# First unit of a differential attention begun before the last tile of the projection in front of it

## The chip, the cores and the metric

One Trainium2 chip, one of its cores. The whole computation is one program; the metric is its time on the device in microseconds, the median of several executions. A change of less than 0.2% (3.9 us here) cannot be told from none with these runs.

## The reference, cut to what matters

Two transformer blocks in fp32 over a sequence of 512 tokens and a width of 1024. The first block (an mLSTM layer and a sparse-attention layer) is not touched. The second block projects the normed input once and feeds two branches from it, an RWKV7 scan and a differential attention:

```python
u = h @ w_in[i]
u_rwkv = u[..., :RWKV_COLS]                       # 1920 columns
u_da = u[..., RWKV_COLS:RWKV_COLS + DA_COLS]      # 1536 columns
...
u = u + mu_prev * (up[:, :-2] - u) + mu_next * (up[:, 2:] - u)      # centred_shift, RWKV columns only
a = sigmoid(a0 + ad @ a2); decay = exp(-exp(-softplus(-(w0 + tanh(wd) @ w2)) - 0.5))
...
lam = exp(sum(lq1 * lk1)) - exp(sum(lq2 * lk2)) + lambda_init
s = einsum('bhcqd,bhckd->bhcqk', q_blk, kt)       # 4 heads, c = 2 score maps, blocks of 128 queries
pr = softmax(s, axis=-1)
pd = pr[:, :, 0] - lam * pr[:, :, 1]
o = einsum('bhqk,bhkv->bhqv', pd, vt)
```

Then come the RWKV scan, both output projections, a feed-forward layer and a gated per-layer embedding.

## The kernel before, in words

Each engine has its own list of instructions, written out in order in Python, and engines meet only at semaphores. `stage_in_2` (the third in-projection) and `stage_da_attention` lie in the same block, so that no barrier stands between them.

**The projection.** The weights stream in as blocks of 256 output columns (the last has 128). ScalarE makes the high part of a block (`split_hi`, L248), VectorE the low part (`split_lo`, L257), and TensorE multiplies 128 columns at a time, a tile, as three products with 24 matmuls (`multiply_tile`). There are 43 tiles, t = 0 to 42; tile number modulo 4 gives the PSUM bank. Tiles t = 28 to 42 are the 15 RWKV tiles, v = 0 to 14. VectorE takes each of these out of its bank with the root of the norm (L2158), releases the bank (L2160), and computes the centred shift in three instructions (L2162, L2163, L2165). The last two tiles are t = 41 (v = 13, bank 2) and t = 42 (v = 14, bank 3), so banks 0 and 1 are free by then.

**What is put between the tiles.** After t = 40 and t = 41 TensorE makes the first head pair's decay and rate products (`first_pass_lora`, L2048), two matmuls each. ScalarE takes their sigmoids (`rw_sigmoids`, L2444), with VectorE's two cumulative scans (`rw_scans`, L2479) in front of the last tile's eviction. GpSimd then multiplies keys by the rate (L2289), and after the wait for `lam` makes sums and differences of the scans (L2294, L2298, L2303) and the key scales (L2308, L2314).

**The attention.** A unit n is a head and a block of 128 queries, 16 in all. TensorE makes both score maps in banks 2 (n mod 2) and the next (`scores`, L2236); VectorE takes both maxima in one reduction (L2382); ScalarE makes both exponentials with their sums (L2351); VectorE inverts the sums (L2394), makes the scalar with lambda (L2395) and the difference of the maps (L2397), which releases TensorE's transposes (L2257), ScalarE's copy (L2358) and the products with V (L2269). VectorE's order is maximum n, then the difference of unit n - 1. TensorE's scores n wait for the exponentials of unit n - 2. Between the units n = 3 to 7 ScalarE makes ten exponentials of the RWKV branch, two at a time, and GpSimd multiplies with them; `beside(m)` lets GpSimd go on only after m differences.

Before the change VectorE's list at the seam reads: eviction 13, shift 13, scans, eviction 14, shift 14, two tiny instructions for `neg_lam` (L2189, L2190), maximum 0, maximum 1, difference 0, maximum 2, difference 1. TensorE's: tile 41, lora 1, tile 42, scores 0, scores 1, scores 2 and so on. ScalarE's: sigmoids 0, sigmoids 1, exponentials 0.

Of the kernel before, what the change touches and what calls it, by code (L numbers as in the profile page):

```python
# [31 lines left out]
DA_HEADS = 4  # L32
# [5 lines left out]
LAMBDA_INIT = 0.8 - 0.6  # L38
# [37 lines left out]
BLOCK_AT, TILE_AT = [], []  # L76
# [1841 lines left out]
RW_ALL = 15  # L1918


def stage_in_2(k, norm):
    nc = k.nc
    b0 = first_block("in_2")
# [22 lines left out]
          "lam_mm", "exp", "copied", "squares", "sums", "floor", "half", "rinv", "wide", "turned", "kkn", "lam", "tanh")}  # L1946
    k.dap, k.rw_done = s, rw_done
    rw_tensors(k)
    first_lora = k.const("cos", S).rearrange("p (m c) -> p m c", m=4)
    k.scan_landed, lora_landed = k.sem("rw_scan_landed"), k.sem("rw_first_lora_landed")  # L1950
    swapped, cleared = [k.sem(f"dap_swapped{i}") for i in range(2)], k.sem("dap_turned_cleared")
# [5 lines left out]
    with k.joined() as block:  # L1957
# [30 lines left out]
        @block.scalar  # L1988
        def _(act):
            split_hi(k, act, b0 + 1)  # L1990
            norm.take_root(act)
            for t, (b, j) in enumerate(tiles):
                if t and j == 0 and b + 1 < b1:
                    split_hi(k, act, b + 1)
                c = t - K0 - 1
                if 0 <= c < RW_T:
                    act.wait_ge(rw_done, made[4 + c])
                    if c >= 2:
                        act.wait_ge(s["sums"], c - 1)
# [80 lines left out]
        def _(dve):  # L2080
# [49 lines left out]
            for t, (b, j) in enumerate(tiles):  # L2130
# [25 lines left out]
                else:  # L2156
                    m = place[v]
                    dve.tensor_tensor(u[:, v % 2, 1:1 + S], bank, norm.root[:], ALU.mult).then_inc(u_ready, 1)  # L2158
                    dve.wait_ge(u_ready, v + 1)
                    dve.sem_inc(k.evac_done, 1)  # L2160
                    x = u[:, v % 2]
                    steps.then_wait(dve, dve.tensor_scalar(t1[:, 0], x[:, 1:1 + S], k.keep[:, m:m + 1], None, ALU.mult))  # L2162
                    steps.then_wait(dve, dve.scalar_tensor_tensor(out=t1[:, 1], in0=x[:, 0:S], scalar=k.col("mu_prev", m),  # L2163
# [21 lines left out]
                    rope(n)  # L2185
                if 8 <= n < 12:
                    value(n - 8)
            dve.wait_ge(s["exp"], 1)
            steps.then_wait(dve, dve.tensor_tensor(prod[:, 4:5], prod[:, 3:4], prod[:, 2:3], ALU.subtract))  # L2189
            dve.tensor_scalar(k.neg_lam, prod[:, 4:5], -LAMBDA_INIT, None, ALU.add).then_inc(s["lam"], 1)  # L2190

def stage_da_attention(k):
    nc = k.nc
    k.da_o = k.region("da_o", [P, TT, S], F32, 74)
    p = k.at("da_p", [P, 3, 2, S], F32, 60)
    pt = k.at("da_pt", [P, 2, S], F32, 72)
    junk = k.region("da_junk", [P, 2, P], F32, 71.25)
    s = {n: k.sem(f"daa_{n}") for n in (  # L2200
          "sc_mm", "nm_done", "exp_done", "pd_done", "tr_mm", "pt", "pv_mm",
          "o_done", "sq_done", "step", "rw_landed", "root", "y_tr", "y_hi", "gate",
          "y_lo", "normed", "omk", "bh")}
    units = [(h, i) for h in range(DA_HEADS) for i in range(TT)]
    U = len(units)
    sumsq = k.small[:, 64:64 + U]
    k.daa, k.da_sumsq = s, sumsq
# [9 lines left out]
    def sm(base, n):  # L2217
        return k.small[:, base + 2 * (n % 4):base + 2 * (n % 4) + 2]

    with k.joined() as block:  # L2220
        @block.sync
# [5 lines left out]

        @block.tensor
        def _(pe):
            def scores(n):  # L2230
                h, i = units[n]
                if n >= 2:
                    pe.wait_ge(s["exp_done"], 2 * (n - 1))
                for c in range(2):
                    rows = rows_half(c)
                    last = pe.matmul(k.ps[:, 2 * (n % 2) + c, :], k.da[rows, h, i * P:(i + 1) * P],  # L2236
                                     k.da[rows, DA_HEADS + h, :], start=True, stop=True)
                last.then_inc(s["sc_mm"], 1)

            pe.wait_ge(k.dap["done"], 8)  # L2240
            pe.wait_ge(k.dap["tr_read"], 4)
            pe.wait_ge(k.evac_done, TILE_AT[b1] - 2)
            scores(0)
            for n in range(U + 3):
                if n == 0:
                    pe.wait_ge(k.evac_done, TILE_AT[b1])
                if n + 1 < U:
                    scores(n + 1)
# [25 lines left out]
        def _(pool):  # L2274
# [66 lines left out]
        def _(act):  # L2341
            exponentials = [x for d in range(2) for x in rw_exponentials(k, act, 0, d)]
            for n in range(U + 4):
                if n < U:
                    act.wait_ge(s["nm_done"], n + 1)
                    if n >= 3:
                        act.wait_ge(s["tr_mm"], n - 2)
                    if n >= 4:
                        act.wait_ge(s["pd_done"], n - 3)
                    for c in range(2):  # L2350
                        act.activation(p[:, n % 3, c, :], k.ps[:, 2 * (n % 2) + c, :], ACT.Exp, bias=sm(0, n)[:, c:c + 1],  # L2351
                                       accum_out=sm(8, n)[:, c:c + 1]).then_inc(s["exp_done"], 1)
                if 2 <= n < U + 2:
                    m = n - 2
                    act.wait_ge(s["tr_mm"], m + 1)
# [15 lines left out]

        @block.vector
        def _(dve):
            steps = Steps(s["step"])
            dve.wait_ge(k.dap["lam"], 1)
            for n in range(U + 4):
                if n < U:
                    bank = 2 * (n % 2)
                    dve.wait_ge(s["sc_mm"], n + 1)
                    if n >= 4:  # L2380
                        dve.wait_ge(s["exp_done"], 2 * (n - 3))
                    dve.tensor_reduce(sm(0, n), k.ps[:, bank:bank + 2, :], AX, ALU.max, negate=True) \  # L2382
                        .then_inc(s["nm_done"], 1)
                if n >= 4:
                    m = n - 4
                    h, i = units[m]
                    dve.wait_ge(s["pv_mm"], m + 1)
                    dve.tensor_scalar(k.da_o[:, i, h * P:(h + 1) * P], k.ps[:, 6 + m % 2, 0:P], sm(24, m)[:, 0:1], None,
                                      ALU.mult).then_inc(s["o_done"], 1)
                if 1 <= n <= U:  # L2390
                    m = n - 1
                    dve.wait_ge(s["exp_done"], 2 * m + 2)
                    x, w = p[:, m % 3], sm(24, m)
                    steps.then_wait(dve, dve.reciprocal(w, sm(8, m)))  # L2394
                    steps.then_wait(dve, dve.scalar_tensor_tensor(out=sm(32, m)[:, 0:1], in0=w[:, 1:2], scalar=k.neg_lam,  # L2395
                                                                  in1=sm(8, m)[:, 0:1], op0=ALU.mult, op1=ALU.mult))
                    dve.scalar_tensor_tensor(out=x[:, 0, :], in0=x[:, 1, :], scalar=sm(32, m)[:, 0:1], in1=x[:, 0, :],  # L2397
                                             op0=ALU.mult, op1=ALU.add).then_inc(s["pd_done"], 1)


def halves():
# [4 lines left out]
def rows_half(x):  # L2406
    return slice(64 * x, 64 * x + 64)
# [1250 lines left out]
```

## Time and profile before

| | |
|---|---|
| median of three runs | 1936.8 us (1934.7 to 1937.28) |
| profiled execution, its own time | 1933.06 us |
| its span, first to last instruction | 1931.1 us |
| mean granted TensorE clock | 0.989 of full speed |
| TensorE matmuls busy | 1851.7 us, 96% of the span |
| VectorE, ScalarE, GpSimd busy | 57%, 36%, 11% |
| the seam of the two stages, last eviction to first transposes | 1088.27 to 1097.68 us |
| the attention's maxima | 1091.6 to 1131.0 us |

The table says how full the engines are over the whole program. The busy shares are means over stages whose limits differ, so that the seam has to be read by itself, engine by engine, in order of time.

### The profile page before, as it was taken

The numbers are of one execution on the slowest core, as the hardware profiler recorded it, in microseconds if no ns is written. First come the engines' busy times: TensorE is split into PE (matmuls) and PEld (weight loads), VectorE is DVE, ScalarE is ACT, GpSimd is POOL, SyncE is SP. The second block draws the span as 40 slices with busy tenths as digits, with TensorE's granted clock in tenths as the row PEclk, the third lists the DMA queues.
The fourth block names the chain that finished last, engine by engine and source line by source line (L and its number), as shares of the span: only waits on it lengthen the run. The fifth ranks groups of instructions, "written<-read, shape, count | busy, mean of one in ns | idle before, by whom it ended". The sixth has DMA issues, their size and how long they took to land. (4 is left out here: it accounts for less than half of the span.)

```text
span 1931.1 us, 35675 instructions
## 1 busy us (share of the span) xinstructions
PE 1851.7 (96%) x15284; PEld 1484.9 (77%) x15284; DVE 1097.6 (57%) x1648; ACT 693.0 (36%) x1154; POOL 221.5 (11%) x221
## 2 busy tenths in 40 slices
PE   8999999999999899999999899999899999999996
PEld 7887757688887666778888568878878888888875
DVE  4664354563256777444366887777465635354534
ACT  4325332341223787442212473423233322122342
POOL 4210011140002000210021340000001000000011
PEclk9999999999999999999999999999999999999998
DMA  5334323152224010124321100002042322322121
GB/s 187 115 109 142 130 77 116 44 209 99 69 69 141 3 45 2 67 92 141 125 100 55 47 2 4 4 3 69 4 175 90 107 98 90 106 92 105 55 98 44
DMA packets 42379, 160.73 MB, mean 83 GB/s; under 512 B 4976, under 2 KB 14192, under 8 KB 27632
## 3 DMA queue, kind: packets, MB, share of 16 engines
q1 hardware_dynamic: 28016, 143.78, 21.7%
q10 hardware_dynamic: 14208, 14.68, 2.1%
q8 instruction: 122, 2.00, 0.4%
q14 instruction: 33, 0.27, 0.0%
HBM read 140.36 MB, written 16.78 MB: 81 GB/s over the span
## 5 line engine op out<-in xcount | busy, mean ns | idle before, releaser
L257 DVE TENSOR_TENSOR wlo<-raw,whi 128x2048 fp32r<-128x2048 f32 (+2 forms) x113 | 251.4, 2225 | 183.9 <-ACT whi L248 183.6
L248 ACT ACTIVATE whi<-raw 128x2048 fp32r<-128x2048 f32 (+2 forms) x113 | 209.0, 1850 | 317.9 <-PE ps L283 161.4
L281 PE MATMUL ps<-act_hi,whi 128*128 128x512 f32 x616 | 243.6, 395 | 0.0
L301 PE MATMUL ps<-act_lo,whi 128*128 128x512 f32 x632 | 242.0, 392 | 0.0
L283 PE MATMUL ps<-act_hi,wlo 128*128 128x512 f32 x616 | 240.8, 391 | 0.0
L282 PE MATMUL ps<-act_lo,whi 128*128 128x512 f32 x616 | 240.7, 391 | 0.0
L300 PE MATMUL ps<-act_hi,whi 128*128 128x512 f32 x592 | 235.5, 398 | 0.0
L305 PE MATMUL ps<-act_hi,wlo 128*128 128x512 f32 x632 | 156.5, 389 | 0.0
L301 PEld LDWEIGHTS ps<-act_lo,whi 128*128 128x128 f32 x632 | 119.7, 189 | 25.6 <-issue 1.2
L305 PEld LDWEIGHTS ps<-act_hi,wlo 128*128 128x128 f32 x632 | 118.6, 188 | 24.6
L300 PEld LDWEIGHTS ps<-act_hi,whi 128*128 128x128 f32 x592 | 111.1, 188 | 32.2 <-issue 8.1
L283 PEld LDWEIGHTS ps<-act_hi,wlo 128*128 128x128 f32 x616 | 116.3, 189 | 24.6
L281 PEld LDWEIGHTS ps<-act_hi,whi 128*128 128x128 f32 x616 | 116.4, 189 | 24.3 <-issue 0.5
L282 PEld LDWEIGHTS ps<-act_lo,whi 128*128 128x128 f32 x616 | 116.2, 189 | 24.1 <-issue 0.5
L3329 PE MATMUL ps<-f_hi,wlo 128*128 128x512 f32 x256 | 99.6, 389 | 0.0
L3328 PE MATMUL ps<-f_lo,whi 128*128 128x512 f32 x256 | 99.6, 389 | 0.0
L3327 PE MATMUL ps<-f_hi,whi 128*128 128x512 f32 x256 | 99.6, 389 | 0.0
L1830 ACT ACTIVATE att_p<-ps,small 128x512 f32<-128x512 f32 (+3 forms) x128 | 66.3, 524 | 28.0 <-DVE small L1871 27.6
L3361 DVE TENSOR_TENSOR xT<-xT,ps 128x512 f32<-128x512 f32 x32 | 21.9, 686 | 82.6 <-PE ps L3329 82.6
L3297 ACT ACTIVATE f_hi<-ff_sq 128x512 fp32r<-128x512 f32 x32 | 20.2, 633 | 123.1 <-DVE ff_sq L3352 123.1
L1871 DVE TENSOR_REDUCE small<-ps 128x2 f32<-128x1024 f32 (+3 forms) x64 | 52.5, 820 | 19.4 <-PE ps L1769 19.2
L1783 PE MATMUL ps<-consts,att_p 128*128 128x128 f32 x320 | 50.7, 285 | 12.0 <-ACT att_p L1837 8.3
(520 smaller groups left out, 3362.0 us busy)
## 6 DMA issues: line engine op xcount, KB each, us to landing
raw<-stream_in SPq DMA_DIRECT2D x107, 1024.0 KB, 4.9
v_scratch<-v_out ACTq DMA_DIRECT2D x16, 256.0 KB, 3.3
z_scratch<-zt ACTq DMA_DIRECT2D x16, 256.0 KB, 2.9
mlh_v<-v_scratch SPq DMA_DIRECT2D x4, 1024.0 KB, 4.8
mlh_z<-z_scratch SPq DMA_DIRECT2D x16, 256.0 KB, 2.6
cmp_w<-cmp_w_in SPq DMA_DIRECT2D x2, 2048.0 KB, 11.3
z_scratch<-in_zt ACTq DMA_DIRECT2D x16, 256.0 KB, 2.2
mix_g<-z_scratch SPq DMA_DIRECT2D x16, 256.0 KB, 6.9
```

Source lines behind the costliest of these rows:

```text
L248: act.activation(k.whi[b % 2][:, 0:n], k.raw[b % RAW_SLOTS][:, 0:n], ACT.Copy).then_inc(k.hi_done, 1)
L257: dve.tensor_tensor(k.wlo[b % 2][:, 0:n], k.raw[b % RAW_SLOTS][:, 0:n], k.whi[b % 2][:, 0:n].bitcast(F32), ALU.subtract).then_inc(k.lo_don ...
L281: pe.matmul(bank, hi, x_hi, start=(x == 0), stop=False)
L282: pe.matmul(bank, hi, x_lo, start=False, stop=False)
L283: last = pe.matmul(bank, lo, x_hi, start=False, stop=(x == end))
L300: pe.matmul(bank, hi, x_hi, start=(x == 0), stop=False)
L301: pe.matmul(bank, hi, x_lo, start=False, stop=False)
L305: last = pe.matmul(bank, lo, x_hi, start=False, stop=(x == end))
L1830: act.activation(p[:, n % 3, e, 0:L], k.ps[:, 2 * (n % 2) + e, 0:L], ACT.Exp, bias=sm(0, n)[:, e:e + 1], accum_out=sm(8, n)[:, e:e + 1]).t ...
L3327: pe.matmul(k.ps[:, t % 4, :], whi, f_hi[:, kt, :], start=(kt == 0), stop=False)
L3328: pe.matmul(k.ps[:, t % 4, :], whi, f_lo[:, kt, :], start=False, stop=False)
L3329: last = pe.matmul(k.ps[:, t % 4, :], wlo, f_hi[:, kt, :], start=False, stop=(kt == KD - 1))
```

## The change

Unit 0 of the attention is begun in the projection. TensorE makes scores 0 after tile 41 and before lora 1, behind waits for the rotated queries and keys, the turned values and the eviction of tile 40. VectorE takes maximum 0 after eviction 13 and before shift 13; `neg_lam` is made after eviction 12; difference 0 and maximum 1 stand between eviction 14 and shift 14. ScalarE makes exponentials 0 between the two pairs of sigmoids, behind a wait for all weight splits, because the tile `da_p` lies over the weight buffers. GpSimd waits for the last tile's matmuls instead of for `lam`. The helper functions are the old bodies of the attention's loops, moved to the top level.

```diff
+def da_weights(k, act, n):
+    act.wait_ge(k.daa["nm_done"], n + 1)
...
+    for c in range(2):
+        act.activation(k.da_p[:, n % 3, c, :], k.ps[:, 2 * (n % 2) + c, :], ACT.Exp, bias=da_small(k, 0, n)[:, c:c + 1],
+                       accum_out=da_small(k, 8, n)[:, c:c + 1]).then_inc(k.daa["exp_done"], 1)
...
@@ stage_in_2, scalar
                     act.wait_ge(k.lo_done, b1 - 2)
+                    if m:
+                        act.wait_ge(k.lo_done, b1)
+                        da_weights(k, act, 0)
                     rw_sigmoids(k, act, 0, m, (4 + 2 * m, 5 + 2 * m))
@@ stage_in_2, tensor
                 multiply_tile(k, pe, b, j, norm if t == 0 else None)
+                if t == K0 + RW_ALL - 2:
+                    pe.wait_ge(s["done"], 8)
+                    pe.wait_ge(s["tr_read"], 4)
+                    pe.wait_ge(k.evac_done, TILE_AT[b1] - 2)
+                    da_scores(k, pe, 0)
@@ stage_in_2, vector
                     dve.sem_inc(k.evac_done, 1)
+                    if v == RW_ALL - 3:
+                        dve.wait_ge(s["exp"], 1)
+                        steps.then_wait(dve, dve.tensor_tensor(prod[:, 4:5], prod[:, 3:4], prod[:, 2:3], ALU.subtract))
+                        dve.tensor_scalar(k.neg_lam, prod[:, 4:5], -LAMBDA_INIT, None, ALU.add).then_inc(s["lam"], 1)
+                    if v == RW_ALL - 2:
+                        da_maximum(k, dve, 0)
+                    if v == RW_ALL - 1:
+                        dve.wait_ge(s["lam"], 1)
+                        da_difference(k, dve, 0)
+                        da_maximum(k, dve, 1)
@@ stage_da_attention, tensor
-            scores(0)
             for n in range(U + 3):
@@ stage_da_attention, gpsimd
-            pool.wait_ge(k.dap["lam"], 1)
+            pool.wait_ge(k.tile_done, TILE_AT[b1])
             past(pool, "scan", 2)
@@ stage_da_attention, scalar
-                if n < U:
+                if 0 < n < U:
@@ stage_da_attention, vector
-                if n < U:
+                if 2 <= n < U:
...
-                if 1 <= n <= U:
+                if 2 <= n <= U:
```

## Rows read from the trace of the kernel before

**Rows 1.** The page, busy time of an engine, share, instructions.

```profile
PE 1851.7 (96%) x15284; PEld 1484.9 (77%) x15284; DVE 1097.6 (57%) x1648; ACT 693.0 (36%) x1154; POOL 221.5 (11%) x221
```

**Rows 2.** By stretch: busy PE, PEld, DVE, ACT, POOL; granted clock, DMA share, GB/s.

```profile
1096.00:1100.00 4.00, 3.29 (x12) 1.17 (x10) 3.93 (x6) 1.93 (x5) 3.77 (x5) 0.72 0.00 2
...
1108.00:1116.00 8.00, 7.34 (x47) 4.68 (x46) 7.79 (x17) 8.00 (x26) 4.11 (x4) 1.00 0.00 0
```

**Rows 3.** Timeline of TensorE over the seam.

```profile
1080.90 1.88 PE L2048 MATMUL ps<-rw,consts 128*128 128x512 f32 x4
...
1088.16 2.04 PE L2236 MATMUL ps<-da 64*128 64x512 f32 x8
1094.34 3.41 PE L2236 MATMUL ps<-da 64*128 64x512 f32 x8 [4.14 <-ACT da_p L2351]
```

**Rows 4.** Timeline of VectorE over the seam.

```profile
1081.10 0.69 DVE L2158 TENSOR_TENSOR in_u<-ps,norm_mix_root 128x512 f32<-128x512 f32 x1 [2.83 <-PE ps L283]
...
1084.94 3.31 DVE L2479 TENSOR_TENSOR_SCAN rw_first_X<-consts,rw_first_sig 128x512 f32<-128x512 f32 x2
1088.27 0.69 DVE L2158 TENSOR_TENSOR in_u<-ps,norm_mix_root 128x512 f32<-128x512 f32 x1
1089.11 0.49 DVE L2162 TENSOR_SCALAR in_t<-in_u,mu_keep 128x512 f32<-128x512 f32 x1
...
1091.20 0.16 DVE L2189 TENSOR_TENSOR da_prod<-da_prod 128x1 f32<-128x1 f32 x1
...
1091.58 2.36 DVE L2382 TENSOR_REDUCE small<-ps 128x2 f32<-128x1024 f32 x2
1094.32 0.17 DVE L2394 RECIPROCAL small<-small 128x2 f32<-128x2 f32 x1 [0.38 <-ACT da_p L2351]
...
1096.58 1.21 DVE L2382 TENSOR_REDUCE small<-ps 128x2 f32<-128x1024 f32 x1
...
1099.24 1.22 DVE L2382 TENSOR_REDUCE small<-ps 128x2 f32<-128x1024 f32 x1
```

**Rows 5.** Timeline of ScalarE over the seam.

```profile
1074.83 1.28 ACT L2444 ACT_TABLE_LOAD   x1 [6.15 <-PE ps L2048]
1076.13 1.26 ACT L2444 ACTIVATE rw_first_sig<-ps,cols 128x512 f32<-128x512 f32 x2
1082.02 1.49 ACT L2444 ACTIVATE rw_rate<-ps,cols 128x512 f32<-128x512 f32 x2 [4.63 <-PE ps L2048]
1083.52 1.28 ACT L2351 ACT_TABLE_LOAD   x1
...
1100.49 0.69 ACT L2351 ACTIVATE da_p<-ps,small 128x512 f32<-128x512 f32 x1 [0.74 <-DVE small L2382]
```

**Rows 6.** By line, duration in ns min/median/max.

```profile
L2165 DVE SCALAR_TENSOR_TENSOR rw<-in_u,cols,in_t x15: 751/752/1661, 1003.5 to 1090.4; 128x512 f32<-128x512 f32 x15
...
L2395 DVE SCALAR_TENSOR_TENSOR small<-small x16: 219/219/1260, 1094.5 to 1134.0; 128x1 f32<-128x1 f32 x16
...
L2397 DVE SCALAR_TENSOR_TENSOR da_p<-da_p,small x16: 750/752/1493, 1095.2 to 1134.2; 128x512 f32<-128x512 f32 x16
```

**Rows 7.** Timeline of VectorE and GpSimd in the projection, of GpSimd over the seam.

```profile
975.78 2.29 DVE L257 TENSOR_TENSOR wlo<-raw,whi 128x2048 fp32r<-128x2048 f32 x1
...
976.01 3.21 POOL L1981 TENSOR_TENSOR da_straight<-da,consts 128x512 f32<-128x512 f32 x1 [4.15 <-DVE da L2100]
...
1082.88 3.18 POOL L2289 TENSOR_TENSOR rw_b<-rw_kkn,rw_rate 128x512 f32<-128x512 f32 x2 [32.51 <-ACT rw_rate L2444]
1091.63 2.48 POOL L2294 TENSOR_TENSOR rw_first_E<-rw_first_X,rw_first_sig 128x512 f32<-128x512 f32 x2 [5.57 <-DVE small L2190]
1094.07 2.04 POOL L2298 TENSOR_TENSOR rw_first_E<-rw_first_X 128x512 f32<-128x512 f32 x2
1096.25 1.52 POOL L2303 TENSOR_TENSOR rw_first_X<-rw_first_E,rw_first_sig 128x512 f32<-128x512 f32 x1
1097.77 2.03 POOL L2308 TENSOR_SCALAR rw_rate<-rw_rate,cols,small 128x512 f32<-128x512 f32 x2
```

More of the change, by code:

```diff
@@ L1918, with da_tensors, da_small, da_scores @@
 RW_ALL = 15
+def da_tensors(k):
+    k.daa = {n: k.sem(f"daa_{n}") for n in (
+          "sc_mm", "nm_done", "exp_done", "pd_done", "tr_mm", "pt", "pv_mm",
+          "o_done", "sq_done", "step", "rw_landed", "root", "y_tr", "y_hi", "gate",
+          "y_lo", "normed", "omk", "bh")}
+    k.da_p = k.at("da_p", [P, 3, 2, S], F32, 60)
+    k.da_steps = Steps(k.daa["step"])
+def da_small(k, base, n):
+    return k.small[:, base + 2 * (n % 4):base + 2 * (n % 4) + 2]
+def da_scores(k, pe, n):
+    h, i = n // TT, n % TT
+    if n >= 2:
+        pe.wait_ge(k.daa["exp_done"], 2 * (n - 1))
+    for c in range(2):
+        rows = rows_half(c)
+        last = pe.matmul(k.ps[:, 2 * (n % 2) + c, :], k.da[rows, h, i * P:(i + 1) * P],
+                         k.da[rows, DA_HEADS + h, :], start=True, stop=True)
+    last.then_inc(k.daa["sc_mm"], 1)
+def da_maximum(k, dve, n):
+    bank = 2 * (n % 2)
+    dve.wait_ge(k.daa["sc_mm"], n + 1)
+    if n >= 4:
+        dve.wait_ge(k.daa["exp_done"], 2 * (n - 3))
+    dve.tensor_reduce(da_small(k, 0, n), k.ps[:, bank:bank + 2, :], AX, ALU.max, negate=True) \
+        .then_inc(k.daa["nm_done"], 1)
+def da_weights(k, act, n):
+    act.wait_ge(k.daa["nm_done"], n + 1)
+    if n >= 3:
+        act.wait_ge(k.daa["tr_mm"], n - 2)
+    if n >= 4:
+        act.wait_ge(k.daa["pd_done"], n - 3)
+    for c in range(2):
+        act.activation(k.da_p[:, n % 3, c, :], k.ps[:, 2 * (n % 2) + c, :], ACT.Exp, bias=da_small(k, 0, n)[:, c:c + 1],
+                       accum_out=da_small(k, 8, n)[:, c:c + 1]).then_inc(k.daa["exp_done"], 1)
+def da_difference(k, dve, m):
+    dve.wait_ge(k.daa["exp_done"], 2 * m + 2)
+    x, w = k.da_p[:, m % 3], da_small(k, 24, m)
+    k.da_steps.then_wait(dve, dve.reciprocal(w, da_small(k, 8, m)))
+    k.da_steps.then_wait(dve, dve.scalar_tensor_tensor(out=da_small(k, 32, m)[:, 0:1], in0=w[:, 1:2], scalar=k.neg_lam,
+                                                       in1=da_small(k, 8, m)[:, 0:1], op0=ALU.mult, op1=ALU.mult))
+    dve.scalar_tensor_tensor(out=x[:, 0, :], in0=x[:, 1, :], scalar=da_small(k, 32, m)[:, 0:1], in1=x[:, 0, :],
+                             op0=ALU.mult, op1=ALU.add).then_inc(k.daa["pd_done"], 1)
 def stage_in_2(k, norm):
@@ L1948, in stage_in_2 @@
     rw_tensors(k)
+    da_tensors(k)
     first_lora = k.const("cos", S).rearrange("p (m c) -> p m c", m=4)
@@ L2187, in _ @@
                     value(n - 8)
-            dve.wait_ge(s["exp"], 1)
-            steps.then_wait(dve, dve.tensor_tensor(prod[:, 4:5], prod[:, 3:4], prod[:, 2:3], ALU.subtract))
-            dve.tensor_scalar(k.neg_lam, prod[:, 4:5], -LAMBDA_INIT, None, ALU.add).then_inc(s["lam"], 1)
 def stage_da_attention(k):
@@ L2196, in stage_da_attention @@
     k.da_o = k.region("da_o", [P, TT, S], F32, 74)
-    p = k.at("da_p", [P, 3, 2, S], F32, 60)
+    p = k.da_p
     pt = k.at("da_pt", [P, 2, S], F32, 72)
     junk = k.region("da_junk", [P, 2, P], F32, 71.25)
[L2200 to L2203, printed above, removed]
+    s = k.daa
     units = [(h, i) for h in range(DA_HEADS) for i in range(TT)]
@@ L2206, in stage_da_attention @@
     sumsq = k.small[:, 64:64 + U]
-    k.daa, k.da_sumsq = s, sumsq
+    k.da_sumsq = sumsq
     b1 = first_block("mix_o")
@@ L2215, in stage_da_attention @@
     k.da_scale = k.small[:, 97:98]
-    def sm(base, n):
-        return k.small[:, base + 2 * (n % 4):base + 2 * (n % 4) + 2]
     with k.joined() as block:
@@ L2229, in _ @@
         def _(pe):
[L2230 to L2242, printed above, removed]
-            scores(0)
             for n in range(U + 3):
@@ L2247, in _ @@
                 if n + 1 < U:
-                    scores(n + 1)
+                    da_scores(k, pe, n + 1)
                 if 2 <= n < U + 2:
@@ L2343, in _ @@
             for n in range(U + 4):
-                if n < U:
[L2345 to L2352, printed above, removed]
+                if 0 < n < U:
+                    da_weights(k, act, n)
                 if 2 <= n < U + 2:
@@ L2373, in _ @@
         def _(dve):
-            steps = Steps(s["step"])
-            dve.wait_ge(k.dap["lam"], 1)
             for n in range(U + 4):
-                if n < U:
[L2378 to L2383, printed above, removed]
+                if 2 <= n < U:
+                    da_maximum(k, dve, n)
                 if n >= 4:
@@ L2387, in _ @@
                     dve.wait_ge(s["pv_mm"], m + 1)
-                    dve.tensor_scalar(k.da_o[:, i, h * P:(h + 1) * P], k.ps[:, 6 + m % 2, 0:P], sm(24, m)[:, 0:1], None,
+                    dve.tensor_scalar(k.da_o[:, i, h * P:(h + 1) * P], k.ps[:, 6 + m % 2, 0:P], da_small(k, 24, m)[:, 0:1], None,
                                       ALU.mult).then_inc(s["o_done"], 1)
-                if 1 <= n <= U:
[L2391 to L2398, printed above, removed]
+                if 2 <= n <= U:
+                    da_difference(k, dve, n - 1)
 def halves():
```

## The prediction

> **What bounds the kernel now.** I read the page first, for the shares: TensorE's matmuls are busy 96% of the span, VectorE 57% and ScalarE 36% [rows 1]. By the page alone, work on VectorE or ScalarE looks free. But the chain of waits that the page follows back covers only the program's last quarter and does not reach the seam, so it says nothing on this change. The timelines of the engines over the seam, one by one, do.
>
> TensorE's timeline shows a hole: it makes scores 0 and 1 from 1088.16, and scores 2 come only after 4.14 us in which it waited for the first exponentials [rows 3]. What is late is seen on VectorE: from 1088.27 it is never idle but for 0.38 us until it reaches maximum 2 at 1096.58. It evicts the last tile, shifts it, makes lambda, and only at 1091.58 starts the first maximum [rows 4]. So VectorE sets the start of the attention. In front of eviction 13 it was idle 2.83 us [rows 4], which is cover. The table by stretch shows who takes over: from 1108 to 1116 ScalarE is busy 8.00 of 8 us, VectorE 7.79 [rows 2]. ScalarE starts exponentials 3 at 1100.49, after a wait of 0.74 for maximum 3 [rows 5], and is nearly full from there. So **the time of maximum 3 (1099.24) is the one to follow**: what it moves, the whole attention moves, and the RWKV stage behind it, which begins with the attention's last products.
>
> **The change, part by part.**
>
> *TensorE.* Two scores cost 2.04, so scores 0 cost 1.02 [rows 3]. They leave the attention and lie in front of lora 1 and the last tile. None of their waits holds: VectorE, idle before eviction 13, had finished all that they ask for. The last tile ends 1.02 later, and with it eviction 14: 1088.27 becomes 1089.29. This price is certain, since TensorE is full up to there. The three table loads by DMA that start at the last tile's end start 1.0 later too; they are wanted only after the last maximum, over 30 us on, so nothing.
>
> *VectorE in front of eviction 14.* Maximum 0 (2.36 / 2 = 1.18 [rows 4]) starts when scores 0 end, about 1082.1, a wait of some 0.2 behind eviction 13, and ends at 1083.3. Queued behind it is shift 13 (2.1 us, as 1089.11 to 1091.20 [rows 4]), to 1085.4, then the scans. Even at the 3.31 that they took here they end at 1088.7, under the last tile's matmuls. So maximum 0 costs nothing where it is put; if that cover failed by more than 0.6 us it would show. Lambda's 0.38 (1091.20 to 1091.58) goes into the idle 2.83: nothing.
>
> *VectorE behind it.* Before, from eviction 14 to maximum 2: 0.84 eviction, 2.09 shift, 0.38 lambda, 2.74 for two maxima and the wait, 2.26 difference 0 (1094.32 to 1096.58), 8.31 in all [rows 4]. After: 0.84 eviction, difference 0 at 2.26, maximum 1 at 1.18, shift 2.09, together 6.37. With the 1.02 later start, maximum 2 is at 1088.27 + 1.02 + 6.37 = 1095.66, **0.92 us earlier**, as long as GpSimd disturbs no more than before.
>
> *ScalarE.* The exponentials need another table than the sigmoids. Before: one load for the sigmoids, one for the exponentials [rows 5]. After: sigmoids 0, load, exponentials 0, load, sigmoids 1, load: two loads more at 1.28 each. The sigmoid load stood idle until lora's product, thus behind a wait of its activation, where the later one ran ahead of its wait [rows 5]; with two waits in front of exponentials 0 as of the sigmoids I let the load follow maximum 0, at 1083.3. Then exponentials 0 run from 1084.6 to 1086.0, a load to 1087.3, the first sigmoid of the rate to 1088.0. Before, GpSimd's first product began at 1082.88 [rows 7]; now at 1088.1. Should the load run ahead, all this is 1.3 us earlier. The third load (1088.8 to 1090.1) lies under the eviction.
> The Trainium skill (ScalarE: Activation LUTs, What ACT_TABLE_LOAD costs) counts 1.28 us and a drain of 1.38 for each switch. The trace does not show the drain: 1074.83 + 1.28 = 1076.11 and the activation starts at 1076.13 [rows 5]. By the page GpSimd would start 2.8 later, with the same clashes one turn on; the sum below would be an estimated +0.5 in place of +1.1.
>
> *GpSimd, and the lock.* This is what eats the gain. GpSimd and VectorE exclude each other: a GpSimd product that started at 976.01, inside the low split of 975.78 to 978.07, took 3.21, against 1.24 for one of two at 1091.63 [rows 7]. The other way, VectorE's operations with two inputs in SBUF waited: L2165 takes 0.75 but 1.66 beside L2289, L2395 0.22 but 1.26, L2397 0.75 but 1.49 [rows 6]. The maxima, which read PSUM, were not stretched (2.36 for two beside L2294 [rows 4, 7]). Before, L2294 waited 5.57 for lambda [rows 7], which stands behind shift 14, so that this shift had VectorE's ports for itself. After, it waits for the last tile only and comes right behind L2289, from about 1090.7. Its run of L2294, L2298, L2303 and L2308 (2.5, 2.0, 1.2, 1.5 undisturbed) now lies on difference 0, shift 14 and difference 1. Turn about: difference 0 ends at 1092.5, as slow as before. Maximum 1 to 1093.7, under L2294's second. Shift 14's first instruction ends at 1094.1; L2298 runs to 1095.1; the second ends at 1095.65; L2298's second runs to 1096.7; the third ends at 1097.25. Shift 14 takes 3.55 in place of 2.09: **+1.46**. Maximum 2 from 1097.3; difference 1 meets both L2308, 2.07 in place of 1.53 (1099.24 - 1096.58 - 1.13): **+0.54**. Maximum 3 at 1100.4.
> The Trainium skill (SBUF — State Buffer, on the shared port pair) has the loser block for the whole instruction. If each of the shift's three operations lost to a fresh 1.26 us one, that would be 3.8 in place of 1.46, and the sum an estimated +3.4.
>
> *Sum at maximum 3:* -0.92 + 1.46 + 0.54 = **+1.1 us**. The profiled execution took 1933.06 around a span of 1931.1, so it would be 1934.2; the median of the runs stands 3.7 above that execution, 1936.8 + 1.1 = **1937.9**.
>
> *Bounds.* Below: no clash on shift 14, and differences 0 and 1 at their free 1.14 (0.17 + 0.22 + 0.75): -0.92 - 1.12 - 0.4 = -2.4. Above: each of the shift's three loses 0.91 (the most of L2165) and difference 1 loses 1.04 + 0.74 in place of 0.4: -0.92 + 2.73 + 1.38 = +3.2.
>
> **The rivals.**
>
> *It gains a little* (0.31). GpSimd's run slips past shift 14, because VectorE holds the ports turn after turn or because L2289 lies elsewhere. For it: in the first kernel most of the 16 differences are at their minimum [rows 6]. Against it: GpSimd was busy without a pause from 1091.63 to 1099.8 [rows 7] and has the same to do. -0.9 to -2.4, 1935.2.
>
> *No change at all* (0.08). ScalarE's full stretch [rows 2] has its own start in its own queue, and a shift of maximum 3 by a microsecond is swallowed there. Against it: it still waited 0.74 for maximum 3 [rows 5]. 1936.8. That scores 0 have to wait after all, so that the change does nothing, is in here too.
>
> *It is slower by more than can be overlooked* (0.06). The clash doesn't end at difference 1: difference 2 loses 1.04 + 0.74 too, against the 0.4 it lost, so +3.2 + 1.4 = +4.6, 1941.4. It decides when VectorE's losses between eviction 14 and maximum 4 are over 5 us more than before. Against it: L2314 waits for differences and so can't start inside one.
>
> *It is faster by more than that* (0.05). TensorE's clock: the granted clock was 0.72 from 1096 to 1100 [rows 2], a mix of 2.4 and 1.2 GHz, after the 4.14 of idleness, and the scores of two units took 3.41 in place of 2.04 [rows 3]. With a shorter hole it could stay at 2.4 GHz: 1.4 more on top of the -2.4, 1933.0. Against it: the wait of TensorE on VectorE hides this today, so those 1.4 are hardly on the path.
>
> **How the numbers follow.** Forecast 0.50: 1937.9, by itself 1936.6 to 1939. The range for 8 in 10 takes in both bounds of the costs, 1934.4 and 1940.0, and some 0.4 for the median of a few runs: 1934.0 to 1940.4. Less than 0.2% of 1936.8 is 3.9 us, about what these runs can tell from no change. Forecast, small gain and no change are all inside: 0.89. Faster 0.05, slower 0.06.
>
> **What would show it.** Eviction 14 at 1.0 later than now, with idleness before it; maximum 0 between eviction 13 and shift 13; three table loads between the first sigmoids and exponentials 1; L2289 begun past 1087; L2294's on shift 14, whose three instructions are stretched to some 3.5 together; maximum 3 about 1 us later. A shift 14 of 2.1 shows me wrong towards the gain. A maximum 0 that pushes the scans past the last tile's end, or a hole in ScalarE behind exponentials 3, would show a step that I left out.

## The result, and the profile after

The change makes the kernel slower: median 1941.06 us over 18 runs against 1936.9 us over 18 runs of the kernel before on the same chip, ratio 1.0023, 95% interval 1.0016 to 1.0030. That is 4.2 us between the medians and 4.4 by the ratio (3.1 to 5.8), about the 3.9 that count as a difference, where 1937.9 (1934.0 to 1940.4) was forecast. The profiled execution took 1941.5 us, span 1939.6, clock 0.986. In the table below, one of e3's eleven executions, at 3102.6 us, is not in its ratio.

All figures below are microseconds counted from the start of eviction 13, the last of VectorE ahead of the change but for the two tiny ones for lambda, which now lie in the idleness in front of it (2.57 for 2.83), so that what lies ahead of it (1080.4 to 1084.5 us, from profile to profile) drops out. "The seam" ends with the attention's last eviction into `da_o`, at 56.62 before and at 60.75 after: **+4.13**, about what the medians differ by. The two profiles differ by another 4.9 behind the seam (793.4 and 798.3), but that part varies from 793.2 to 800.1 over the profiles of all kernels here, without an order that this change would explain.

VectorE's timeline after, from eviction 13 to maximum 5 (after the time: duration, line, operation, output<-inputs, shapes, and in brackets idleness and who ended it). It answers to [rows 4].

```profile
1080.59 0.69 DVE L2222 TENSOR_TENSOR in_u<-ps,norm_mix_root 128x512 f32<-128x512 f32 x1 [2.57 <-PE ps L283]
1081.66 1.22 DVE L1951 TENSOR_REDUCE small<-ps 128x2 f32<-128x1024 f32 x1 [0.38 <-PE ps L1941]
...
1089.04 0.69 DVE L2222 TENSOR_TENSOR in_u<-ps,norm_mix_root 128x512 f32<-128x512 f32 x1 [1.81 <-PE ps L305]
1090.30 0.17 DVE L1969 RECIPROCAL small<-small 128x2 f32<-128x2 f32 x1 [0.56 <-DVE in_u L2222]
1090.50 1.16 DVE L1970 SCALAR_TENSOR_TENSOR small<-small 128x1 f32<-128x1 f32 x1
1091.69 1.72 DVE L1972 SCALAR_TENSOR_TENSOR da_p<-da_p,small 128x512 f32<-128x512 f32 x1
1093.33 1.21 DVE L1951 TENSOR_REDUCE small<-ps 128x2 f32<-128x1024 f32 x1
1094.46 1.12 DVE L2236 TENSOR_SCALAR in_t<-in_u,mu_keep 128x512 f32<-128x512 f32 x1
1095.62 1.63 DVE L2237 SCALAR_TENSOR_TENSOR in_t<-in_u,cols,in_t 128x512 f32<-128x512 f32 x1
1097.29 1.14 DVE L2239 SCALAR_TENSOR_TENSOR rw<-in_u,cols,in_t 128x512 f32<-128x512 f32 x1
1098.67 1.23 DVE L1951 TENSOR_REDUCE small<-ps 128x2 f32<-128x1024 f32 x1 [0.23 <-DVE rw L2239]
...
1100.92 1.22 DVE L1951 TENSOR_REDUCE small<-ps 128x2 f32<-128x1024 f32 x1
...
1103.55 1.22 DVE L1951 TENSOR_REDUCE small<-ps 128x2 f32<-128x1024 f32 x1 [0.29 <-PE ps L1941]
1106.29 0.35 DVE L2425 TENSOR_SCALAR da_o<-ps,small 128x128 f32<-128x128 f32 x1 [1.52 <-PE ps L2320]
```

Between eviction 14 and maximum 3 (20.33 after eviction 13; 18.14 before) no idleness of VectorE names another engine: its own operations are long. L1970 takes 1.16 where it needs 0.22, L1972 1.72 for 0.75, and the shift's three 1.12, 1.63, 1.14 for 0.48, 0.75, 0.75. Behind maximum 3 it is the other way: its operations are short again and it waits 0.29 and 1.52 for TensorE. The two parts need two causes. GpSimd's timeline has the first; it answers to [rows 7]:

```profile
1087.90 2.51 POOL L2340 TENSOR_TENSOR rw_b<-rw_kkn,rw_rate 128x512 f32<-128x512 f32 x2 [38.03 <-ACT rw_rate L2474]
1090.37 2.48 POOL L2345 TENSOR_TENSOR rw_first_E<-rw_first_X,rw_first_sig 128x512 f32<-128x512 f32 x2
1092.81 2.49 POOL L2349 TENSOR_TENSOR rw_first_E<-rw_first_X 128x512 f32<-128x512 f32 x2
1095.44 1.26 POOL L2354 TENSOR_TENSOR rw_first_X<-rw_first_E,rw_first_sig 128x512 f32<-128x512 f32 x1
1096.70 2.38 POOL L2359 TENSOR_SCALAR rw_rate<-rw_rate,cols,small 128x512 f32<-128x512 f32 x2
```

It runs from 1087.90 to 1099.1 almost without a pause, over all five of the stretched operations, and ends before difference 1 (1099.81). The second cause is in the table by stretch, which answers to [rows 2] (busy PE, PEld, DVE, ACT, POOL; then the granted clock), and in TensorE's timeline, which answers to [rows 3]:

```profile
1092.00:1096.00 4.00, 0.00 (x0) 0.00 (x0) 3.96 (x4) 1.43 (x4) 3.86 (x4) 1.00 0.99 409
1096.00:1100.00 4.00, 2.52 (x8) 1.01 (x8) 3.69 (x4) 0.09 (x2) 3.07 (x3) 0.59 0.04 17
1100.00:1104.00 4.00, 2.58 (x7) 1.07 (x8) 3.60 (x7) 3.31 (x9) 1.93 (x2) 0.50 0.00 0
1104.00:1108.00 4.00, 4.00 (x19) 2.85 (x18) 2.41 (x6) 2.97 (x7) 0.60 (x1) 0.63 0.00 0
```

```profile
1096.07 1.48 PE L1941 MATMUL ps<-da 64*128 64x512 f32 x4 [4.24 <-ACT da_p L1962]
1097.48 1.11 PE L2308 MATMUL ps<-consts,da_p 128*128 128x128 f32 x4
1101.42 2.08 PE L1941 MATMUL ps<-da 64*128 64x512 f32 x4 [2.83 <-ACT da_p L1962]
1103.43 1.11 PE L2308 MATMUL ps<-consts,da_p 128*128 128x128 f32 x4
1104.34 1.91 PE L2320 MATMUL ps<-da_v,da_pt 128*128 128x128 f32 x8
1106.18 1.50 PE L1941 MATMUL ps<-da 64*128 64x512 f32 x4
...
1109.09 1.13 PE L1941 MATMUL ps<-da 64*128 64x512 f32 x4
...
1111.63 0.70 PE L1941 MATMUL ps<-da 64*128 64x512 f32 x2
```

TensorE stands idle 4.24, works 2.5, stands idle 2.83. From about 1096.7 to 1107.0, 10.2 us, it is at 1.2 GHz (0.50). There one unit takes it 4.76 from scores to scores (1101.42 to 1106.18), against 2.54 at 2.4 GHz (1109.09 to 1111.63). VectorE's own pace is 2.51 a unit (maximum 4 at 20.77 to maximum 5 at 23.28, before). At 2.4 GHz the two are level; at 1.2 GHz TensorE sets the pace.

The second hole ends with the exponentials of unit 2, which had waited for maximum 2 (1098.67).

ScalarE went as the prediction laid it out:

```profile
1082.98 1.28 ACT L1962 ACT_TABLE_LOAD   x1 [6.09 <-DVE small L1951]
...
1085.74 1.28 ACT L2474 ACT_TABLE_LOAD   x1
1087.04 1.27 ACT L2474 ACTIVATE rw_rate<-ps,cols 128x512 f32<-128x512 f32 x2
1088.32 1.28 ACT L1962 ACT_TABLE_LOAD   x1
```

### The profile page after: what moved, and what is told of

Read it like the earlier page. It is cut to its first block and busy times, and to the rows that moved or that the text cites. A ratio compares the mean times of both kernels' runs of the same rounds, so it can differ in the third digit from the quotient of the medians.

```text
span 1939.6 us, 35677 instructions
## 1 busy us (share of the span) xinstructions
PE 1855.8 (96%) x15284; PEld 1487.6 (77%) x15284; DVE 1098.1 (57%) x1648; ACT 695.5 (36%) x1156; POOL 221.4 (11%) x221
```

## The experiments

The table has what each run showed. The first three columns are of one profile each: maximum 3, the rest of the seam behind it, and the end. The last is the ratio to the kernel before, with its 95% interval; 0.001 is 1.9 us.

| kernel | to max 3 | from there | end | ratio |
|---|---|---|---|---|
| before | 18.14 | 38.48 | 56.62 | |
| before, again | 18.14 | 38.49 | 56.63 | 1.0001 [0.9992, 1.0011] |
| after | 20.33 | 40.42 | 60.75 | 1.0023 [1.0016, 1.0030] |
| after, again | 20.33 | 40.79 | 61.12 | one run, 1942.9 |
| e1 GpSimd behind shift 14 | 18.05 | 40.16 | 58.21 | 1.0007 [0.9998, 1.0016] |
| e2 sigmoids first | 20.13 | 39.56 | 59.69 | 1.0018 [1.0009, 1.0026] |
| e3 after, filler | 20.34 | 38.92 | 59.26 | 1.0021 [1.0012, 1.0029] |
| e4 before, GpSimd early | 20.25 | 38.48 | 58.73 | 1.0008 [0.9998, 1.0018] |
| e5 after, no reads | 16.51 | 38.48 | 54.99 | 0.9995 [0.9985, 1.0004] |
| e6 before, no reads | 17.35 | 38.48 | 55.83 | 1.0002 [0.9991, 1.0013] |
| e7 before, filler | 18.16 | 38.50 | 56.66 | 1.0012 [1.0003, 1.0022] |
| e9 one beside each | 16.50 | 40.36 | 56.86 | 1.0003 [0.9992, 1.0013] |
| e10 e1 and filler | 18.05 | 41.20 | 59.25 | one run, 1934.9 |
| e11 e9 and filler | 16.50 | 39.16 | 55.66 | 1.0005 [0.9994, 1.0016] |

**e1. When GpSimd starts.**

```diff
-            pool.wait_ge(k.tile_done, TILE_AT[b1])
+            pool.wait_ge(k.rw_done, RW_ALL)
```

> The changed kernel, with GpSimd's sums and differences of the scans held back until shift 14 is done (they waited for the last tile's matmuls). Theory 'lock': VectorE's maximum 2 is late because shift 14 takes turns with GpSimd at the shared ports; then shift 14 falls from 3.97 to about 2.1 us, maximum 2 comes some 2 us earlier, and of the 4.2 us of loss at least 2 go. Theory 'clock' adds that TensorE's waits become shorter, so that the stretch at 1.2 GHz gets shorter and 3 to 4 us go. Theory 'bare cost' (scores in front of the last tile, 1.0 us, and two more table loads, 2.6 us): nothing changes, 4 us stay.

With GpSimd's run begun only behind shift 14, difference 0 and the shift take their free times and maximum 2 is at 14.25 (15.48 before, 18.08 after). Then the rest of the run lies on differences 1 to 3; of difference 1:

```profile
1097.44 1.02 DVE L1970 SCALAR_TENSOR_TENSOR small<-small 128x1 f32<-128x1 f32 x1
1098.49 1.49 DVE L1972 SCALAR_TENSOR_TENSOR da_p<-da_p,small 128x512 f32<-128x512 f32 x1
```

The seam is 2.54 shorter than after's but still 1.59 longer than before's: the clash has moved, not gone. Its part behind maximum 3 (40.16) holds the losses of differences 2 and 3, and 1.2 GHz lasts 3.4 us, all of it ahead of maximum 3.

**e2. The table loads.** Both pairs of sigmoids in front of exponentials 0, so that ScalarE loads two tables in place of four.

```diff
+                    rw_sigmoids(k, act, 0, m, (4 + 2 * m, 5 + 2 * m))
                     if m:
                         act.wait_ge(k.lo_done, b1)
                         da_weights(k, act, 0)
-                    rw_sigmoids(k, act, 0, m, (4 + 2 * m, 5 + 2 * m))
```

> The changed kernel, with both pairs of sigmoids in front of exponentials 0, so that ScalarE loads two tables in place of four. Theory 'bare cost' (the table loads): 2.6 us of the 4.2 us come back. Theory 'lock': GpSimd's first product moves from 1087.9 to about 1084, so that difference 0 no longer meets it, but the sums and differences start at the last tile's end, 1089, and meet difference 0 and the first half of shift 14 in its place; VectorE loses nearly as much, 0 to 1.5 us come back. Theory 'clock': the waits of TensorE stay over 4 us, so the slow stretch stays; no more than 1.5 us back.

GpSimd's first product is early again (1084.86), as before the change, but its next ones come behind the scans and the last tile (1090.49) and lie on the same five operations. Maximum 3 gains 0.20, the end 1.06. So the loads are not what makes maximum 3 late. The other 0.86 lies behind it, where TensorE was at 1.2 GHz for 10.2 us, as in after; 0.37 of such a difference can be chance (e8 below), and the rest is not explained.

**e3 and e7. TensorE's clock.** Matmuls of constants, which nothing reads, in the holes: ten after (six in front of scores 3, four in front of scores 4), six before (in front of scores 2).

```diff
+            def filler(count):
+                pe.wait_ge(k.rw_ss["sigs"], 4)
+                for _ in range(count):
+                    pe.matmul(k.ps[:, 7, :], k.const("ident"), k.const("sin", S), start=True, stop=True)
...
+                if n in (2, 3):
+                    filler((0, 0, 6, 4)[n])
```

> The changed kernel with ten more matmuls of constants into an idle bank, six in front of scores 3 and four in front of scores 4, where TensorE waits for ScalarE; nothing reads them. Theory 'clock': the granted clock doesn't fall to 1.2 GHz between 1097 and 1106, the scores, transposes and products with V of the first units take 1.1, 0.7 and 1.1 us again, and about 1.9 us of the 4.2 come back; maximum 3 is where it was. Theory 'lock' alone: VectorE sets the pace and nothing comes back. 'Bare cost': nothing comes back. If the ten matmuls are longer than the waits that they fill, it is slower by the excess, at most 2 us.

> The kernel before with six matmuls of constants into an idle bank in front of scores 2, in TensorE's hole of 4.1 us; nothing reads them. Theory 'clock': the stretch at 1.2 GHz from 1095 to 1098.5 goes, and the attention gets at most 0.5 us shorter, because in this kernel VectorE, not TensorE, sets the pace through that stretch. If it gets 1.5 us or more shorter, the clock cost the kernel before as much as the changed one, and the clock explains none of the difference. Theory 'lock' alone: no change beyond 0.3 us.

The clock stays at 2.4 GHz in both. In e3:

```profile
1096.00:1100.00 4.00, 4.00 (x10) 1.71 (x9) 3.96 (x4) 1.45 (x4) 3.86 (x4) 1.00 0.99 398
1100.00:1104.00 4.00, 4.00 (x15) 1.72 (x14) 3.69 (x5) 0.17 (x1) 2.98 (x3) 1.00 0.02 9
1104.00:1108.00 4.00, 4.00 (x18) 1.77 (x17) 3.79 (x7) 3.37 (x10) 2.04 (x2) 1.00 0.00 0
```

After, maximum 3 doesn't move (20.34), and the part behind it falls from 40.42 to 38.92: 1.50 of the 1.94 come back. The fillers themselves are too long, 5.42 in the hole of 4.24 and 3.60 in that of 2.83, which may hold the rest. Before, the same cure gives nothing (56.66 for 56.62), as the prediction said of the kernel before. Its fillers too are longer than the hole (5.42 for 4.14), which could have eaten a small gain; but in before's own trace VectorE shows no wait for TensorE between eviction 14 and maximum 5, so that its time at 1.2 GHz is under VectorE's work. So the clock costs nothing before and some 1.5 after. The medians do not confirm a gain for either (below).

**e4. The new line of GpSimd alone**, in the kernel before.

```diff
-            pool.wait_ge(k.dap["lam"], 1)
+            pool.wait_ge(k.tile_done, TILE_AT[b1])
```

> The kernel before, with only the one line for GpSimd changed: its sums and differences wait for the last tile's matmuls and not for lambda. Theory 'lock': shift 14 goes from 2.1 to 3.5 to 4 us, the first maximum is that much later, and the kernel is 1.5 to 2 us slower; with 'clock' it may be 3. Against it, GpSimd is done sooner, so that difference 0 and difference 1 lose less than now, which gives back up to 1 us. 'Bare cost': no change, because neither the tile nor the table loads move.

+2.11 at maximum 3 and at the end. Shift 14's instructions show it:

```profile
1090.10 0.85 DVE L2162 TENSOR_SCALAR in_t<-in_u,mu_keep 128x512 f32<-128x512 f32 x1
1090.98 1.63 DVE L2163 SCALAR_TENSOR_TENSOR in_t<-in_u,cols,in_t 128x512 f32<-128x512 f32 x1
1092.65 1.41 DVE L2165 SCALAR_TENSOR_TENSOR rw<-in_u,cols,in_t 128x512 f32<-128x512 f32 x1
```

This one line, with the old order of everything else, costs about as much as the whole change does up to maximum 3 (+2.19). But not all of it is the clash. Differences 0 and 1 are free here, and VectorE then waits for scores 2, which TensorE makes at 1.2 GHz:

```profile
1097.95 3.79 PE L2236 MATMUL ps<-da 64*128 64x512 f32 x8 [6.76 <-ACT da_p L2351]
1100.08 1.22 DVE L2382 TENSOR_REDUCE small<-ps 128x2 f32<-128x1024 f32 x1 [0.94 <-PE ps L2236]
```

TensorE is at 1.2 GHz for 6.8 us, twice as long as before, and yet the part behind maximum 3 is 38.48 as before: how long the slow stretch lasts does not set the cost, but what it lies on.

**e5 and e6. The seam without the clash.** In both kernels eleven operations of GpSimd's (the products, sums and key scales up to `rw_kd`) are replaced by a memset of the same tile, which reads nothing and takes 0.5 in place of 1.2; the RWKV branch's first head pair thus gets constants. For one of them:

```diff
-                last = pool.tensor_tensor(E1[:, d, :], X[:, d, :], sig[:, d, :], ALU.subtract)
+                last = pool.memset(E1[:, d, :], 0.5)
```

> The changed kernel, with GpSimd's nine instructions between the sigmoids and the features (the products with the rate, sums and differences of the scans, key scales, scaled keys) replaced by fills of the same tiles with a constant, so that the RWKV branch is left out of the result; the fills read nothing and are short. It says what the change is worth where the ports are free. Counted from eviction 13 to the last eviction of the attention, which was 56.6 us before and 60.8 after. Theory 'lock': differences 0 to 3 and shift 14 at their free durations; maximum 2 at about 13.7 us behind eviction 13 (15.5 before), the last eviction at 53 to 55, and less than in the next kernel by some 1 us, the head start. Theory 'clock' alone: TensorE's hole between scores 2 and 3 stays at 2 us or more, and the stretch at 1.2 GHz stays; the gain over the changed kernel is under 2 us. 'Bare cost': the changed kernel stays about 2 us or more behind the next one.

> The kernel before with the same fills in place of the same nine instructions: the other half of the comparison. Theory 'lock': differences 0 to 2 lose the 1.9 us that they lost to GpSimd, so the attention's last eviction is at about 54.5 to 55 us behind eviction 13 in place of 56.6, and the changed kernel with fills is some 1 us better. 'Bare cost': this one is 2 us or more better than the changed one with fills.

In e5 nothing is stretched. The memsets lie beside difference 0 and maximum 1, and are over at 1092.8, so that shift 14 has nothing beside it:

```profile
1090.63 0.22 DVE L1970 SCALAR_TENSOR_TENSOR small<-small 128x1 f32<-128x1 f32 x1
1090.89 0.75 DVE L1972 SCALAR_TENSOR_TENSOR da_p<-da_p,small 128x512 f32<-128x512 f32 x1
...
1092.69 0.48 DVE L2236 TENSOR_SCALAR in_t<-in_u,mu_keep 128x512 f32<-128x512 f32 x1
1093.20 0.75 DVE L2237 SCALAR_TENSOR_TENSOR in_t<-in_u,cols,in_t 128x512 f32<-128x512 f32 x1
1093.99 0.75 DVE L2239 SCALAR_TENSOR_TENSOR rw<-in_u,cols,in_t 128x512 f32<-128x512 f32 x1
```

So the change of order by itself is worth 16.51 - 17.35 = -0.84 at maximum 3, and -0.84 at the end. (At the end only where the clock stays up: e9 below has the same times up to maximum 3 and ends at 56.86.) The clash costs 18.14 - 17.35 = 0.79 before, and 20.33 - 16.51 = 3.82 after. For e6 an end at 54.5 to 55 was expected, and 55.83 came: without its own losses VectorE waits for scores 2, made at 1.2 GHz, so that of some 1.5 of losses only 0.79 come back.

```profile
1096.27 1.23 DVE L2380 TENSOR_REDUCE small<-ps 128x2 f32<-128x1024 f32 x1 [0.66 <-PE ps L2236]
```

The five stretched operations of after account for those 3.82 one by one: 0.94 + 0.97 + 0.64 + 0.88 + 0.39. The DMA transfers that start with the last tile's end are no rival: from 1092 to 1096 the DMA share was 1.01 in e5, with nothing stretched, and 0.99 in after. The clock didn't fall in e5 at all, and the part behind maximum 3 is 38.48, as before.

**e8 and e12. The same kernels again.**

> The changed kernel once more, for one look: do the seam's times repeat? From eviction 13 maximum 2 at 18.1, maximum 5 at 27.1, the last eviction of the attention at 60.8 us, and the granted clock at half from 1097 to 1106.5. If they repeat within 0.3 us, a reading of one profile of the seam is good to that; if the stretch of half clock lies elsewhere or has another length, the 1.7 us between maximum 3 and maximum 5 are chance.

> The kernel before once more, as a measure of what the comparison and one profile can tell. The seam (eviction 13 to the attention's last eviction) is set by the order of the engines and should be 56.6 us again within 0.4, the clock at 1.2 GHz for some 3.5 us in it. What lies ahead of eviction 13 (1081.1 us in the first profile) and behind the attention (793.4) I expect to differ by up to 3 and 6 us, as it did between the other profiles, since it holds stretches at 1.2 GHz that come and go. Ratio 1.0000 with an interval of about 0.001 to each side. If the seam itself moved by more than a microsecond, the differences of 1 to 2 us between the experiments would mean nothing; if the ratio lay outside 0.999 to 1.001, neither would the medians.

The seam repeats to 0.01 before and to 0.37 after, all of it behind maximum 3, where TensorE was at 1.2 GHz for 13.6 us in e8 and for 10.2 in after. That is a little more than the 0.3 that e8 allowed. Differences of a microsecond between seams mean something, as far as two pairs of profiles can tell. The ratio of before to itself is 1.0001, with an interval of 0.001 to each side, so that the timed runs tell apart 4 us and not 1 us.

**e9, e10 and e11. Towards a better version.** e9 is after with e2's order, and with GpSimd's run cut up, one product beside each reduction from PSUM or eviction, which weren't stretched (`beside(n)` waits for difference n - 1). e10 is e1 with e3's ten fillers. e11 is e9 with five fillers, three and two.

```diff
+            pool.tensor_tensor(E1[:, 1, :], X[:, 1, :], sig[:, 1, :], ALU.subtract)
...
+            beside(1)
+            to_end(1)
+            pool.wait_ge(k.rw_done, RW_ALL)
+            past(pool, "e2", 1)
             pool.tensor_tensor(X[:, 1, :], E2[:, 1, :], sig[:, 1, :], ALU.add).then_inc(ss["sums"], 1)
+            beside(2)
+            pool.tensor_tensor(E1[:, 0, :], X[:, 0, :], sig[:, 0, :], ALU.subtract).then_inc(ss["e1"], 1)
+            beside(3)
+            to_end(0)
...
+            beside(4)
```

> The changed kernel, with the same work for GpSimd in another order and behind other waits, so that each instruction of its run falls beside a maximum or an eviction, which don't use the shared ports: sigmoids 1 in front of exponentials 0 (two table loads less), the first difference of the scans beside eviction 14, then one instruction after each of VectorE's differences, the sum beside maximum 2, the features three units later than before. Nothing is left out. Theory 'lock': no instruction of VectorE is stretched between eviction 14 and maximum 8, so maximum 2 is at 14.3 us behind eviction 13 and the attention's last eviction near the 55.0 of the kernel with fills, at most 55.8; against 56.6 before and 60.8 changed. With 'clock': no stretch at 1.2 GHz, since TensorE's holes are 2 us. The program 1 to 1.5 us faster than before, which these runs can hardly show, and 5 us faster than the change. If GpSimd's last instructions, now behind the last difference, hold up the RWKV stage, the gain is gone again there.

> The changed kernel with GpSimd held back until shift 14 is done and with the ten matmuls of constants in TensorE's holes. Theory 'clock' as a separate cost: the 3.5 us at 1.2 GHz that stayed in the kernel with the hold alone go, and at most 0.5 us of its 58.2 with them, since VectorE's own losses (1.5, 0.9 and 1.9 us on differences 1 to 3) set its pace. If it falls by 1.5 us as in the changed kernel with fillers, the clock costs the same whatever VectorE does. If the fillers are longer than TensorE's holes here (2.3 us for six matmuls of 4 us), it is slower instead, by up to 1.5 us.

> The kernel of e9_one_beside_each, with three constant matmuls in front of scores 3 and two in front of scores 4, whose results nothing reads. In e9 TensorE stood at 1.2 GHz from 1094.5 to 1101 and the seam lasted 56.86 us from eviction 13 to the attention's last eviction, though VectorE lost nothing up to maximum 3 (16.50 us). A matmul of 128 by 512 took 0.66 in e3_filler at 1.2 GHz and less at 2.4, so that three are about 1.4 us and two about 0.9, under the holes of e9 (2.3 and 1.7 us). If the clock is the rest of the loss: granted clock 1.00 or close to it from 1094 to 1102, maximum 3 at 16.5 us as in e9, maximum 5 at 21.3 to 21.8 in place of 22.87, last eviction at 55.0 to 55.6, thus 1.0 to 1.6 us under the kernel before (56.62), a ratio near 0.9995 which the interval can't tell from 1. If the clock is only a companion of something else (the order of GpSimd, an exponential): the clock is full and maximum 5 stays at 22.5 to 22.9, last eviction at 56.5 or later. If the fillers are too few to hold the clock: it falls again to 0.5 for several us and the seam stays as in e9.

e9 takes the whole clash away between eviction 14 and maximum 3: maximum 3 at 16.50, as in e5, with GpSimd's products computed. Yet the part behind it is 40.36, where the end was expected at 55.0 to 55.8 and no stretch at 1.2 GHz. e11 shows most of why; first e9, then e11:

```profile
1096.00:1100.00 4.00, 3.23 (x10) 1.22 (x8) 3.74 (x8) 3.14 (x8) 1.72 (x3) 0.50 0.15 61
1100.00:1104.00 4.00, 4.00 (x23) 3.06 (x22) 2.62 (x6) 3.04 (x9) 1.00 (x1) 0.75 0.00 0
```

```profile
1096.00:1100.00 4.00, 4.00 (x20) 2.00 (x19) 3.89 (x7) 3.69 (x11) 1.99 (x2) 1.00 0.01 4
1100.00:1104.00 4.00, 4.00 (x25) 2.24 (x24) 3.86 (x10) 3.91 (x13) 1.85 (x3) 1.00 0.00 0
```

With the clock held, 1.20 comes back, and e11's seam is 55.66, 0.96 shorter than before's. Its ratio, 1.0005 [0.9994, 1.0016], doesn't show this. What e11's expectation says of e9 and of the price of a filler was misread: e9 was at 1.2 GHz from 1095.1 to 1102.0, the clock never fell in e3's seam, and one such matmul takes two instructions of 0.592 each, one every 0.45 or so, so that e11's three took 2.84 (not 1.4) and its two 1.88 (not 0.9). In e10 the fillers were longer than the holes that e1 leaves: maximum 3 to 4 takes 4.72 in place of e1's 3.10, with 1.53 of waiting for TensorE, and the seam is 1.04 longer than e1's. So e10 can't tell what the clock costs there.

## Why the prediction was wrong, step by step

**The step that failed: TensorE's clock.** The prediction had the clock as a way to gain only, and held that "those 1.4 are hardly on the path". That is true of before, as e7 shows. But the prediction itself lengthened VectorE's stretch between maxima 1 and 2, behind which come the exponentials that TensorE waits for, and did not ask what this does to TensorE: a second hole of 2.83 behind the first, and 1.2 GHz for 10.2 us in place of 3.4, now over units that also have transposes and products with V. There a unit takes TensorE 4.76 against VectorE's 2.51. Part behind maximum 3: +1.94, not in the sum and in no rival. The filled holes of e3, after in all else, show 1.50 of it to be the clock; e9 and e11 show 1.20 of 1.88 in another kernel. What the other 0.44 in after is isn't shown. With the sum's error of 1.11 at maximum 3, which comes next, this makes the +4.13 where +1.1 was forecast. It was foreseeable: [rows 3] had the scores of two units at 3.41 for 2.04, and a whole unit of three such parts at half the clock against VectorE's pace would have shown the bound changing hands.

**The head start, -0.92.** Measured without the clash, -0.84 (e5 less e6). But two errors cancel in it. After has idleness that I left out: eviction 14 is 1.28 later, not 1.02; from its end to difference 0 are 0.56, where 0.15 had been in front of the shift; 0.23 stands in front of maximum 2. That is 0.26 + 0.42 + 0.23 = 0.91. On the other side e6's maximum 2 waits 0.66 for TensorE, at 1.2 GHz, and some 0.17 is in the length of single operations. That -0.84 came so near is luck. The idleness of 0.56 and 0.23 is the same in e1, e5, e9 and e11, so it is neither the clash nor the clock; which of the waits takes it isn't shown.

**GpSimd and the lock, +1.46 and +0.54.** Right in kind and place for shift 14: GpSimd's first product at 1087.90 (1088.1 forecast), the run right behind it, shift 14 at 3.97 (3.55 forecast). Difference 0 took 3.03 and not "as slow as before", 2.26; difference 1 was free, 1.11, and not 2.07, since GpSimd had finished. Summed over the three, the clash was put at 3.51 (1.12 + 1.46 + 0.93 above the free times) and came to 3.82. The size was off by 0.3 only, but because too little on difference 0 and shift 14 was made up by too much on difference 1. The Trainium skill (SBUF — State Buffer, on the shared port pair) lets the loser block for the other's whole instruction; the estimate by it was +3.4 at maximum 3, the turns worked out from the rows gave +1.1, and +2.19 was measured, between them. The page's other half, that VectorE operations with two inputs are held up only against a GpSimd operation that reads SBUF, agrees with e5's difference 0, which memsets did not hold up (0.22 and 0.75).

**At maximum 3** the sum was +1.1 and +2.19 was measured. The difference of 1.11 is 0.91 of idleness and of the later eviction, and 0.23 of durations (+0.77 on difference 0, +0.42 on shift 14, -0.96 on difference 1), less some 0.03 in the maxima. Then come the 1.94 behind it: 4.13.

**ScalarE.** Right in each step: load behind maximum 0 at 1082.98 (1083.3 forecast), exponentials at 1084.28, load, sigmoids at 1087.04. The drain that the Trainium skill (ScalarE: Activation LUTs, What ACT_TABLE_LOAD costs) counts behind a load is again not seen: 1085.74 + 1.28 = 1087.02, and the sigmoid starts at 1087.04.

**The rivals.** The slow one, a clash that goes on to difference 2, gave 1941.4 and 0.06; the time came out there, but by another mechanism: differences 1 and 2 were free, and from eviction 14 to maximum 4 VectorE took 0.91 longer than before, not over 5. The small gain (0.31) needed GpSimd's run to slip past shift 14; e1 made it do so, and it was slower still by 1.59, because the run then lay on differences 1 to 3. No change at all (0.08) failed, since the end moves with maximum 3: by 2.11 for 2.11 in e4, by 0.84 for 0.84 from e6 to e5. The gain by a clock that stays (0.05) needed a shorter hole, and the holes were 4.24 and 2.83 for 4.14.

**What stays open.** Why the clock fell in e9 and e1 and not in e5 isn't known. In all three scores 3 begin 13.58 behind eviction 13, after the same hole of 2.34, and the clock then went to 1.2 GHz for 6.8 us, for 3.4 us and not at all. So the same idleness does not always bring the same clock, and part of what after lost to it may be a matter of chance; its second profile lost as much or more (+2.31). Nor is what the rest of the program does: behind the seam the profiles differ by up to 7 us (793.2 to 800.1), with stretches at 1.2 GHz that come and go: for after 17.1 us of them in the 320 us behind the seam, in its second profile 10.3, before 10.2 and 6.8. The three timed kernels with fillers have ratios that are 1.4, 2.3 and 1.9 us above what their seams say (e3, e7, e11), the others 1.2 at most; whether fillers cost something later is a suspicion, since each such number is uncertain by some 2 us, and e10's one profile, with fillers, had the shortest rest of all (793.2). So no version here is shown to beat the kernel before.

## What to carry to other kernels

Where a change lengthens what TensorE waits for, work out its next unit at the half clock and compare it with the pace of the engine that now sets the time. If the half-clock unit is longer, as 4.76 against 2.51 here, each hole can cost twice. A chain of VectorE operations beside an unbroken run of GpSimd products lost on five of its seven operations here, a tiny one among them; the reciprocal (0.17) and the maximum from PSUM lost nothing. So place GpSimd's products one by one beside reductions from PSUM, which e9 showed to be free up to maximum 3, and look at where the run ends before you move its start. For effects of 1 us in 1900, measure from a landmark to a landmark inside the profile, since medians of ten runs didn't resolve them here.

## What had not been expected of the hardware

An operation of 128 by 1 elements, 0.22 by itself, took 1.02 to 1.27 beside GpSimd's products in after, e1, e2 and e3, and 0.60 to 0.64 in before: it can be held up by as much as an operation of 512 columns, and its own size says nothing on its price. L2236, with one tile and one column as inputs, was held up as well (1.12, and 1.53 in e2, for 0.48), which the sum had not priced. And the clock stayed at 1.2 GHz for 10.2 and 13.6 us in after's two profiles, though TensorE was busy for all of 1104 to 1107 in the first.
